# ScalarE rounds tile s + 3, not s + 4, behind the GELU of tile s, up to the last u tile

## The reference, cut to what matters

```python
def peer(x, w_q, sub_keys, u, v):              # T = 512 tokens, D = 1024
    def block(xb):                             # 128 tokens
        qb = (xb @ w_q).reshape(TOKEN_BLOCK, PEER_HEADS, 2, PEER_DKEY)
        s = jnp.einsum('thcd,hcnd->thcn', qb, sub_keys)
        s_top, i_top = lax.top_k(s, PEER_TOPK)           # 16 of 128, per half
        ...                                              # 16 of the 256 sums, softmax -> g, eidx
        ug = jnp.take(u, eidx, axis=0)
        vg = jnp.take(v, eidx, axis=0)
        h = jax.nn.gelu(jnp.einsum('td,thkd->thk', xb, ug), approximate=False)
        return jnp.einsum('thk,thkd->td', (g * h).astype(x.dtype), vg)
```

## Time and profile before

| | us |
|---|---|
| median of three runs | 1604.93 (1602.98 to 1606.12) |
| the profiled execution | 1601.73 |
| its span in the trace | 1599.9 |
| PE busy | 1578.9 (99%) |
| DVE busy | 1276.5 (80%) |
| ACT busy | 630.1 (39%) |
| POOL busy | 533.3 (33%) |

### The profile page before, as it was taken

One profiled execution on the slowest core, in us unless ns is written; L12 is line 12 of the kernel. 1 busy time (PEld: TensorE's weight loads), 2 busy tenths in 40 slices (PEclk: granted clock), 3 DMA queues, 4 the chain that ended last, 5 costly groups with the idle time before them and its releaser, 6 DMA issues.

```text
span 1599.9 us, 24488 instructions
## 1 busy us (share of the span) xinstructions
PE 1578.9 (99%) x9566; PEld 1393.4 (87%) x9566; DVE 1276.5 (80%) x2390; ACT 630.1 (39%) x996; POOL 533.3 (33%) x261
## 2 busy tenths in 40 slices
PE   9999999999999999999999999999999999999998
PEld 7897977888989999989999998888878888888886
DVE  3024366345899999999998879999989999999997
ACT  5424345532222333445555333333334433434332
POOL 4433223351235789421010233333332232232200
PEclk9999999999999999999999999999999999999999
DMA  5332212135123669699998899999999999999972
GB/s 202 143 145 80 70 54 80 60 108 175 53 93 121 181 185 319 217 332 319 354 341 280 290 418 405 405 414 409 405 388 422 417 410 411 394 389 420 405 286 76
DMA packets 141633, 427.05 MB, mean 267 GB/s; under 512 B 11344, under 2 KB 73040, under 8 KB 120272
## 3 DMA queue, kind: packets, MB, share of 16 engines
q1 hardware_dynamic: 118224, 274.47, 47.5%
q0 software_dynamic: 23296, 151.04, 23.5%
HBM read 378.77 MB, written 46.14 MB: 266 GB/s over the span
## 4 chain that ended last, share of the span: by engine, by line
PE 62%; DVE 29%; DMA 4%; issue 3%; ACT 1%; POOL 0%; SPq 0%; DVEq 0%; ACTq 0%
PE bank L1437 19%; PE bank L1438 18%; PE bank L1439 18%; DVE acc L1311 4%; DVE uvb L1273 4%; DVE wlo L1265 3%; PE bank L1743 3%; DMA raw<-in_u 3%; DVE idx L1179 1%; DVE idx L1171 1%; DVE val L1170 1%; DVE val L1178 1%; DVE tmp L1172 1%; DVE cand L1214 1%; DMA raw<-in_uv 1%
## 5 line engine op out<-in xcount | busy, mean ns | idle before, releaser
L1437 PE MATMUL bank<-xhi,whi 128*128 128x352 f32 (+1 forms) x1408 | 488.5, 347 | 5.0 <-ACT hout L917 2.8
L1438 PE MATMUL bank<-xlo,whi 128*128 128x352 f32 (+1 forms) x1408 | 481.1, 342 | 0.0
L1439 PE MATMUL bank<-xhi,wlo 128*128 128x352 f32 (+1 forms) x1408 | 480.7, 341 | 0.0
L714 POOL DMA_INDIRECT uvb<-in_uv,eidx x128 | 212.1, 1657 | 551.5 <-DVE acc L1311 400.7
L896 ACT ACTIVATE whi<-raw 128x1024 fp32r<-128x1024 f32 x255 | 268.8, 1055 | 202.7 <-PE bank L1439 133.9
L1265 DVE TENSOR_TENSOR wlo<-raw,whi 128x1024 fp32r<-128x1024 f32 x215 | 262.6, 1222 | 52.9 <-ACT whi L896 52.6
L1437 PE MATMUL bank<-whi,ahi 128*128 128x512 f32 x762 | 300.1, 394 | 2.0 <-DVE wlo L1265 2.0
L1439 PE MATMUL bank<-whi,alo 128*128 128x512 f32 x762 | 297.4, 390 | 0.0
L1438 PE MATMUL bank<-wlo,ahi 128*128 128x512 f32 x762 | 297.2, 390 | 0.0
L1437 PEld LDWEIGHTS bank<-xhi,whi 128*128 128x128 f32 x1408 | 265.1, 188 | 22.2 <-DVE wlo L1265 4.4
L1439 PEld LDWEIGHTS bank<-xhi,wlo 128*128 128x128 f32 x1408 | 265.6, 189 | 15.4
(11 more groups left out here) (225 smaller groups left out, 1858.8 us busy)
## 6 DMA issues: line engine op xcount, KB each, us to landing
raw<-in_u SPq DMA_DIRECT2D x128, 512.0 KB, 6.5
raw<-in_uv SPq DMA_DIRECT2D x127, 512.0 KB, 9.7
g_scratch<-stage SPq DMA_DIRECT2D x48, 512.0 KB, 6.8
gl<-g_scratch SPq DMA_DIRECT2D x32, 768.0 KB, 8.7
raw<-in_w_in SPq DMA_DIRECT2D x22, 1024.0 KB, 4.8
h_scratch<-hout SPq DMA_DIRECT2D x96, 192.0 KB, 5.4
hl<-h_scratch SPq DMA_DIRECT2D x24, 768.0 KB, 11.5
raw<-in_w_q SPq DMA_DIRECT2D x6, 1024.0 KB, 4.8
```

Source lines behind the costliest of these rows:

```text
L714: nc.gpsimd.indirect_dma_start(out=uvb[:, r % UVB, :], out_offset=None, in_=a["uv"][:, :], in_offset=bass.IndirectOffsetOnAxis(ap=eidx[:, ...
L1437: mm(out, lh, rh, start=first, stop=False)
L1438: mm(out, lh, rl, start=False, stop=False)
L1439: return mm(out, ll, rh, start=False, stop=last)
```

## The change

Before, behind the GELU of tile s ScalarE rounds tile s + 4, for all s. Now nothing is rounded at s = 0, tile s + 3 is rounded for s = 1 to 154 (`LAST_U`), and at s = 154 tile s + 4 as well; from s = 155 on it is tile s + 4 again. The number of instructions is the same on every engine.

```diff
@@ -128,6 +128,9 @@
     at_step = U_POS[v_tile(p)] + 4 if p < FUSED else V_POS[p] - 1
     PRODUCT_STEP.append(max(PRODUCT_STEP[-1:] + [at_step]))
+
+
+LAST_U = U_POS[NT - 1]
@@ -944,7 +947,10 @@
                     gelu(n)
                 elif n < NT - LAST:
                     act.wait_ge(v_done, n + 1)
-                tile_high(s + 4)
+                if 1 <= s <= LAST_U:
+                    tile_high(s + 3)
+                if s >= LAST_U:
+                    tile_high(s + 4)
                 for q in quads_after(s):
                     g_evac(q)
```

## The result

| | before | after |
|---|---|---|
| median, us | 1605.53 (1602.98 to 1606.83, 4 runs) | 1748.41 (1746.14 to 1750.99, 4 runs) |
| ratio | | 1.090 (95%: 1.088 to 1.092) |
| span of the profiled execution | 1599.9 | 1745.6 |

The change costs 143 us, 9%. The forecast was 1741 us, with 1710 to 1782 as its range.

The account below looks back on a forecast made before the run. TensorE, busy 99%, was taken as the bound, VectorE setting the mixed stage's pace. 84.1 + 5.3 + 37 + 2 + 8 = 136.4 us on 1601.7 gave 1738.1, the median 3.2 higher: 1741 us, range 1710 to 1782.

Parts of the forecast that it names:

- start, up to tile 48: Steps 0 to 47: later rounding delays POOL's low parts, VectorE's selection work takes part back; 2 us, between 0 and 4.
- G steps, tile 48 to 88, with the clock: VectorE's lead shrinks by a tile, so TensorE waits for one-hots: 37 us, plus 8 for clock falls.
- the step into step 91: Step 91 must wait for the rounding behind tile 88's GELU, beginning at 906.13 instead of 900.85: 5.3 us.
- steps 91 to 155: VectorE idles ahead of low parts, waiting for roundings; it needs 360.7 us where it took 276.6: 84.1 us added.
- v stage: Behind step 155 the order is the old one and VectorE is busy 92%, so nothing is given back.
- Mixed stage: New VectorE gaps of 1.98 us after products, 1.32 after dots; a pair of steps takes 11.51 us, not 8.21.
- The loop of 10.36 and 12.66 us: G steps: GELU, rounding, VectorE's step, one-hots, next tile; 10.36 us per two tiles, 12.66 with dots, against TensorE's 9.66.
- The rival by which VectorE's lead of over two tiles covers the loss: G steps cost nothing because VectorE leads TensorE by over two tiles; only the mixed stage pays: 1696 us, 10%.
- The clock: TensorE's clock may fall behind waits in ten dot rounds of the G steps: 0 to 17 us, half taken, 8.
- the rival with TensorE at its lower clock throughout: Mixed stage: TensorE stays at the lower clock, a pair takes 14.3 us, 78 us more: 1819 us, 7%.
- The faster rival: GELUs no longer stand behind roundings with late loads, giving back two waits and two clock falls, 8.2 us: 1597 us, 2%.

Follow-up runs that it names:

- the answers a step back: The change, with ScalarE's dot-product GELU and product rounding for VectorE's step s + 2, not s + 3, in steps 1 to 154: 1657.45 us.
- the G steps alone: The change on steps 47 to 87 only, the old order elsewhere, against the kernel before: 1653.86 us, ratio 1.030.
- The repair of the G steps: The change with HOT_LEAD = 1 in place of 2, so the one-hots are due a tile later: 1693.65 us, ratio 1.057.
- only `dots_gelu` back: The change, with only the GELU of the dot products a step back in ScalarE's queue, the product's rounding staying: 1711.03 us, ratio 1.068.
- the run with the start alone: The change on steps 0 to 46 only, the old order elsewhere, against the kernel before: 1605.73 us, ratio 1.0018.
- The last experiment: Kernel before with HOT_LEAD = 1, plus the change and ScalarE's answers to VectorE a step back in steps 90 to 96 only: 1599.28 us, ratio 0.9981.
- the two runs with the answers a step back: The change with ScalarE's answers to VectorE a step later in its queue, without and with HOT_LEAD = 1: 1657.45 and 1604.00 us.
- the run of steps 88 to 154 alone: The change on steps 88 to 154 only, the old order elsewhere, against the kernel before: 1695.24 us, ratio 1.057.
- With `HOT_LEAD = 1`: The kernel before with HOT_LEAD = 1 in place of 2, one-hots due a tile later: 1598.39 us, ratio 0.9982.

## Why the prediction was right, point by point

The forecast of 1741 us lies 7 us below the 1748 measured. Its mechanism was right in both large terms; the G steps with their clock term were 7.6 us too cheap. The terms of the sum, measured from the start of a tile or low part in both traces (705.1 is the start of tile 48 after, 700.8 before, and so on):

| term | forecast, us | in the trace, us |
|---|---|---|
| start, up to tile 48 | 2 | 4.3 |
| G steps, tile 48 to 88, with the clock | 37 + 8 | 52.6 |
| the step into step 91 | 5.3 | 5.3 |
| steps 91 to 155 | 84.1 | 84.5 |
| v stage | 0 | -1.0 |
| sum | 136.4 | 145.7 |

*Mixed stage.* The gaps were forecast as 1.98 and 1.32 us and a pair as 11.51; the rows show 1.89 and 1.22 in brackets (start to start, 1.97 and 1.30, from what VectorE's next instruction would have been) and 11.50. The 25 pairs from step 105 took 287.4 us of 287.8. The mechanism is shown, not argued: with the answers a step back the stage gave back 88.5 us, all of the 84.5 and a little more.

The 84.5 is a net figure. The new waits sum to more, 99.0 us, as the prediction said they would; before, VectorE idled there for 16.1 us, most of it in steps 91 to 97, where a late load held it once for 5.7 us. In the changed kernel steps 91 to 98 took the forecast's 8.93 us a pair, so the slower loop hid that. The forecast comes out right because it took its 360.7 against the old 276.6, which holds these stalls; of the late loads in these steps it named only TensorE's wait at tile 94.

*G steps.* The loop of 10.36 and 12.66 us holds. Where no clock fall lies, a round of three tiles with a dot step took 801.35 - 783.87 = 17.48 us in the changed kernel (starts of tiles 63 and 60), forecast 17.49, and four such rounds in the other slowed kernels took 17.47 or 17.48. TensorE's wait in it is 0.56 + 2.15 us, where one of 2.4 was forecast. That the count of rounds came out near is in part luck. Nine dot rounds lie between tiles 48 and 88, not ten, since the one-hots of step 49 are due behind tile 47: 3.0 us less. The last tiles cost more: from tile 75 on 9.1 us and not 4, of which 5.0 in the four tiles with the wide batches, which the prediction priced like plain ones; and its own terms there, ten times 0.35 and 1.4 for a double batch, make 4.9, not 4. Steps 54 and 60 have two batches too, and were left out. The rival by which VectorE's lead of over two tiles covers the loss is out: this part alone cost 51.9 us.

*The clock* is the term that was mis-sized, by taking half of the ten falls. Granted clock and matmuls of the changed kernel in one of its low stretches, which began in the last microsecond of a wait of 2.85 us for one-hots, ended at 761.37 (us, PE, PEclk, DMA share, GB/s):

```profile
760.70:767.40 6.70, 6.03 (x31) 0.50 1.04 359
```

Between tiles 48 and 88 the clock was at half for 27.3 us in all, seven stretches, which takes up to 13.7 us of matmul time; I had taken 8. That leaves 39 us for the loop. The repair of the G steps can't tell the two apart, since it removes the waits and the falls together (clock 1.00, stretch 199.9 us). Four kernels with the same G steps can, as their falls differ: at half clock for 22.3, 25.7, 27.3 and 32.6 us, they took 249.0, 250.6, 252.4 and 253.8 us (in this order: only `dots_gelu` back, the G steps alone, the change, both answers back). The shortest and the longest, in the columns of the stretches above:

```profile
704.60:953.60 249.00, 213.83 (x1717) 204.50 (x1715) 187.69 (x270) 103.24 (x172) 16.58 (x17) 0.96 0.79 251
704.70:958.50 253.80, 217.88 (x1717) 208.53 (x1714) 188.05 (x270) 104.12 (x173) 16.55 (x17) 0.94 0.77 246
```

A line through the four rises by 0.48 us for each us at half clock and meets 238.6 us at none, an estimate from beyond the points. So nearly every microsecond that the clock could take was paid, because the loop passes through TensorE, and the loop without it costs some 39 us.

In the mixed stage the clock fell too, ten times for 3.4 us from step 100 on (0.95 over the stretch), and cost nothing: from step 105 on the pairs with a fall and those without took the same 11.50 us. TensorE waited up to 0.8 us at one tile and 1.7 to 2.2 at the next, and had the time:

```profile
1158.13 0.43 PE L1443 MATMUL bank<-xhi,whi 128*128 128x352 f32 x1 [0.83 <-DVE wlo L1271]
1164.43 0.50 PE L1443 MATMUL bank<-whi,ahi 128*128 128x512 f32 x1 [2.15 <-DVE wlo L1271]
```

So the rival with TensorE at its lower clock throughout is out. The Trainium skill (TensorE: Matmul & The Clock Gate, the section on oscillation in real kernels) tells of a kernel that is throttled anew in every round, behind waits for transfers of 3 to 5 us. The trace agrees in part: there is a wait in each of some 27 pairs, of 1.6 to 2.7 us and so shorter than those, and a fall in ten of them. The prediction read more out of that section than it says: a fall in each round is not a clock that stays down, and it does not follow that the falls cost time.

*Start.* 4.3 us and not 2, in the profiled execution. TensorE was held by POOL at tiles 29 to 31 for the full delay of about a tile (tile 31 starts at 629.0 against 624.9), and VectorE's late end of the selection gave back 1.6 us of it by tile 43 as expected; the rest came at tiles 46 to 48, where the one-hots were late already and the clock fell for 6.8 us. In the run with the start alone, whose trace has no fall there, tile 48 was 2.4 us late. By the medians that run cost 3.8 us.

*The faster rival.* It asked for a rounding that never blocks a GELU. The last experiment shows that even with VectorE's waits out of the way there is nothing to win at tile 95, since the GELU waits for a store in the same spell. At tile 155 the two runs with the answers a step back tried it: the rounding, asked for a step later, still found its load late, by 4.50 and 3.56 us (4.89 before), and TensorE waited 1.93 us in the one and 0.98 in the other, and there 1.31 again a few tiles on (1.97 before). The second of them:

```profile
1176.56 1.06 ACT L899 ACTIVATE whi<-raw 128x1024 fp32r<-128x1024 f32 x1 [3.56 <-DMA raw<-in_uv]
```

## What to carry to other kernels

Where two in-order engines feed each other, look at what stands between an answer and the next thing that the other engine needs. An instruction moved one step back in such a queue can end up behind a wait for the very engine that waits for it, and then the price is the full round trip, each time (here 1.3 or 2.0 us), with both engines less than 75% busy. Price a shorter lead as a loop: add the steps from release to due time and compare them with the tiles between; slack in busy shares or in a neighbouring buffer's lead says nothing of it.

## What the runs showed of the hardware

In the G steps the granted clock was at half for seven stretches, 27.3 us, where I had counted on five of 3.4. Six of them began close to one of the eight waits of 2.1 to 2.9 us, the seventh in a wait of 1.45 us, and two waits of 2.15 us (at 881.7 and 956.1) had none. In the mixed stage a wait of 1.6 to 2.7 us came in every pair, and only ten falls. The same waits can bring a fall in one execution and none in another: at tile 46 TensorE waited 1.27 and 1.46 us both in the kernel before and in the run of steps 88 to 154 alone, and only the second shows a fall there, 3.4 us.

A fall cost nearly its full half in the G steps, where the bound passes through TensorE (0.48 us for each us), and nothing in the mixed stage, where VectorE and ScalarE set the pace (11.50 us a pair with and without).

With `HOT_LEAD = 1` there is a spell of late transfers between 910 and 935 us in which loads and stores are both late: in one order of its queue ScalarE waited 8.21 us for a load, in the other 8.10 us for a store. What makes them late stays open.
